# Half of the first modulation rows summed on TensorE, and the second modulation row of each chunk queued behind the weights

## The chip, the cores and the metric

The kernel runs on one core of a Trainium2 chip. The metric is the device time of one execution in microseconds; lower is better. TensorE (PE in the rows) multiplies matrices, VectorE (DVE), ScalarE (ACT) and GpSimd (POOL) do elementwise work, and SyncE (SP) issues the loads. Each engine runs its own program in order and waits on semaphores for the others.

## The reference

Two transformer blocks follow each other on x of 256 rows by 1024 columns. Each has a gated feed-forward (FFN), an attention mix and another FFN. Every normalised input is scaled and shifted by vectors ("modulation") that are themselves a product of a small vector with a large matrix:

```
mods = (silu(c) @ w_ada + b_ada).reshape(B, 9, 1024)      # w_ada: 1024 x 9216
n = rmsnorm(h, g_pre[0]) * (1 + scale(0)) + shift(0)
f = (silu(n @ w_gate) * (n @ w_up)) @ w_down              # 1024 x 2816, 1024 x 2816, 2816 x 1024
h = h + 0.5 * gate(0) * rmsnorm(f, g_post[0])
```

The first FFN can't start before shift(0) and scale(0) are there: 2048 columns of w_ada, 8 MB. The other modulation vectors of the first block are worked out during that FFN.

## The kernel before, in words

All matrices are float32. To get near-float32 results out of the faster float32r matmuls, each weight piece is split in two, hi (ScalarE copies with rounding) and lo = raw - hi (VectorE subtracts), and so is the activation nT. A product is then three matmuls, hi by hi, hi by lo and lo by hi. `split_hi` (ACT, L838) and `split_lo` (DVE, L1228) do this for a piece of 128 x 2048, which takes two loads of 512 KB.

An FFN is cut into 11 chunks of 256 hidden columns. Stage F0 is the first FFN. For chunk c TensorE multiplies piece (0, c), that is rows 0 to 511 of gate and up, then piece (1, c), rows 512 to 1023, and then the down piece of the chunk before. Pieces lie in four buffers (A = w_raw 0, B = 1, D = 2, E in the arena); `lo_ready` of a buffer tells SyncE that it may be loaded again and TensorE that it may be used.

The opening is written out by hand (`opening` on TensorE, `first_rows`, `first_fold`, `first_folded` and `first_out` on VectorE, `load_first` on SyncE). It works in two halves of 512 columns of shift and scale. Half 0 is needed for rows 0 to 511 of the FFN's weights, half 1 for rows 512 to 1023. For a half there are eight modulation rows (j = 0 to 7) of 128 x 1024, 512 KB each. A row is multiplied by the column `c_act[:, 0, j]` and added up; the sum over partitions and the turn into columns comes from a fold (DVE reduce, L1516) and one matmul with a constant, `pick` (L2133). VectorE sums all eight rows of half 0 and six of half 1. The other two rows of half 1 (`ON_PE = [2, 3]`) are summed on TensorE by `first_row_sums`: eight matmuls a row with the 128 x 128 block of the row as weights and one moving column (L2140), put between the weight matmuls three at a time behind one tile of chunk 0 and then one at a time in piece (0, 1). When `first_mods` says that a half's shift and scale are ready, the transposed x is scaled into nT (ACT L865, DVE L1251) and split. x is transposed on TensorE (L1950).

During F0, `load_ada` queues two modulation rows a chunk, 128 x 3072 and 1.5 MB each (ada 0 and ada 1), and VectorE multiplies and adds them (L1317, L1320). In the loop both are queued behind the down piece and ahead of the next chunk's gate and up pieces, and both are added ahead of their splits.

## Time and profile before

| | us |
|---|---|
| median of 3 runs | 1088.44 |
| lowest and highest | 1088.26, 1089.09 |
| the profiled execution | 1088.02 |
| its span | 1086.3 |
| TensorE busy in the span | 1057.0 |
| VectorE, ScalarE busy | 854.4, 549.7 |

The span is the time from the first to the last instruction that the profiler saw; 1.7 us of the execution lie outside of it. A busy TensorE is one that has a matmul in flight; it says nothing about how densely the matmuls follow each other, which one reads from their start times.

### The profile page before, as it was taken

How to read it: one execution, taken by the hardware profiler on the slowest of the kernel's cores; microseconds unless marked ns; L12 is line 12 of the kernel's file. 1: busy time of each engine (PE TensorE's matmuls, PEld its weight loads, DVE VectorE, ACT ScalarE, POOL GpSimd, SP SyncE). 2: the span in 40 equal slices, each digit the busy share in tenths (PEclk: the TensorE clock that was granted, in tenths of full speed). 3: DMA queues.
4: the chain of work that ended last, by engine and by line, in shares of the span. 5: the costliest groups of instructions: out<-in, count | busy, mean ns of one | idle time of the engine just before them, and what ended most of it. 6: DMA issues, size and time to landing. Idle time of an engine off the chain costs nothing.

```text
span 1086.3 us, 16196 instructions
## 1 busy us (share of the span) xinstructions
PE 1057.0 (97%) x6136; PEld 924.2 (85%) x6136; DVE 854.4 (79%) x932; ACT 549.7 (51%) x669; POOL 47.6 (4%) x78
## 2 busy tenths in 40 slices
PE   3999999999999999999999999999999999999997
PEld 2999999889988788888978888898887778888886
DVE  6899888678887888887778988877876787666665
ACT  4444343564765754444565444445654456444452
POOL 1000000011120100000010000000100000000001
PEclk9999999999999999999999999999999999999999
DMA  9999997466424598997669999854563536767651
GB/s 340 382 403 389 389 394 265 152 157 218 150 78 155 194 336 309 320 311 239 206 235 350 344 369 339 278 174 136 179 206 104 194 118 226 233 214 231 216 174 59
DMA packets 147140, 265.26 MB, mean 244 GB/s; under 512 B 9769, under 2 KB 104470, under 8 KB 141974
## 3 DMA queue, kind: packets, MB, share of 16 engines
q1 hardware_dynamic: 145376, 261.30, 69.7%
q0 software_dynamic: 1056, 3.17, 1.0%
q8 instruction: 30, 0.49, 0.2%
q10 hardware_dynamic: 662, 0.16, 0.1%
q14 instruction: 16, 0.13, 0.0%
HBM read 263.34 MB, written 1.27 MB: 244 GB/s over the span
## 4 chain that ended last, share of the span: by engine, by line
PE 90%; DVE 4%; ACT 2%; DMA 1%; issue 1%; SPq 1%; POOL 1%; POOLq 0%; DVEq 0%; ACTq 0%
PE ps L1999 18%; PE ps L1930 12%; PE ps L1931 12%; PE ps L1932 12%; PE ps L2005 9%; PE ps L1980 7%; PE ps L1982 6%; PE ps L1983 6%; DMA arena<-in_w_ffn_up 1%; ACT w_hi L838 1%; PE ps L2474 1%; DVE x_res L1405 1%; DVE nT L1251 1%; DVE y_row L1399 0%; PE ps L2293 0%
## 5 line engine op out<-in xcount | busy, mean ns | idle before, releaser
L1228 DVE TENSOR_TENSOR w_lo<-w_raw,w_hi 128x2048 fp32r<-128x2048 f32 (+1 forms) x163 | 367.1, 2254 | 103.3 <-ACT w_hi L838 102.5
L838 ACT ACTIVATE w_hi<-w_raw 128x2048 fp32r<-128x2048 f32 (+2 forms) x169 | 317.5, 1884 | 245.4 <-PE ps L1932 96.4
L1999 PE MATMUL ps<-nT_both,w_hi 128*128 128x512 f32 x864 | 210.7, 391 | 0.0
L1999 PEld LDWEIGHTS ps<-nT_both,w_hi 128*128 128x128 f32 x864 | 158.8, 188 | 30.7
L1980 PE MATMUL ps<-nT_both,w_hi 128*128 128x256 f32 x576 | 164.3, 285 | 0.0
L1982 PE MATMUL ps<-nT_both,w_hi 128*128 128x256 f32 x576 | 162.9, 283 | 0.0
L1983 PE MATMUL ps<-nT_both,w_lo 128*128 128x256 f32 x576 | 162.9, 283 | 0.0
L1320 DVE SCALAR_TENSOR_TENSOR arena<-arena,c_act 128x3072 f32<-128x3072 f32 (+2 forms) x49 | 129.4, 2651 | 0.4 <-DMA arena<-in_ada_w 0.4
L1930 PE MATMUL ps<-w_hi,hT_hi 128*128 128x512 f32 x320 | 125.0, 391 | 0.0
L1931 PE MATMUL ps<-w_lo,hT_hi 128*128 128x512 f32 x320 | 125.0, 390 | 0.0
L1932 PE MATMUL ps<-w_hi,hT_lo 128*128 128x512 f32 x320 | 124.5, 389 | 0.0
L2005 PEld LDWEIGHTS ps<-nT_both,w_lo 128*128 128x128 f32 x864 | 114.3, 191 | 6.3
L2005 PE MATMUL ps<-nT_both,w_lo 128*128 128x256 f32 x864 | 116.3, 282 | 0.0
L1980 PEld LDWEIGHTS ps<-nT_both,w_hi 128*128 128x128 f32 x576 | 110.4, 192 | 0.7
L1982 PEld LDWEIGHTS ps<-nT_both,w_hi 128*128 128x128 f32 x576 | 110.5, 192 | 0.4
L1983 PEld LDWEIGHTS ps<-nT_both,w_lo 128*128 128x128 f32 x576 | 110.4, 192 | 0.0
L1930 PE MATMUL ps<-w_hi,nT_both 128*128 128x512 f32 (+2 forms) x236 | 91.4, 387 | 0.1
L1932 PE MATMUL ps<-w_hi,nT_both 128*128 128x512 f32 (+2 forms) x236 | 89.7, 380 | 0.0
L1931 PE MATMUL ps<-w_lo,nT_both 128*128 128x512 f32 (+2 forms) x236 | 89.6, 380 | 0.0
L1932 PEld LDWEIGHTS ps<-w_hi,hT_lo 128*128 128x128 f32 x320 | 60.1, 188 | 12.8
L1930 PEld LDWEIGHTS ps<-w_hi,hT_hi 128*128 128x128 f32 x320 | 60.2, 188 | 11.4
L1931 PEld LDWEIGHTS ps<-w_lo,hT_hi 128*128 128x128 f32 x320 | 60.2, 188 | 11.0
(310 smaller groups left out, 1239.8 us busy)
## 6 DMA issues: line engine op xcount, KB each, us to landing
arena<-in_w_ada SPq DMA_DIRECT2D x16, 1536.0 KB, 9.4
arena<-in_ada_w SPq DMA_DIRECT2D x16, 1536.0 KB, 8.2
w_raw<-in_w_in SPq DMA_DIRECT2D x44, 512.0 KB, 4.5
w_raw<-in_ffn_w_down SPq DMA_DIRECT2D x44, 512.0 KB, 4.1
w_raw<-in_w_ffn_gate SPq DMA_DIRECT2D x42, 512.0 KB, 7.0
w_raw<-in_w_ffn_up SPq DMA_DIRECT2D x42, 512.0 KB, 8.2
w_raw<-in_w_ffn_down SPq DMA_DIRECT2D x42, 512.0 KB, 4.5
w_raw<-in_ffn_w_gate SPq DMA_DIRECT2D x42, 512.0 KB, 4.2
```

Of the source, the lines that this page charges most:

```text
L838: copy = lambda o, i: act.activation(o, i, ACT.Copy)
L1228: dve.tensor_tensor(lo(s, n), raw(s, n), hi(s, n).bitcast(F32), ALU.subtract).then_inc(lo_ready[s], 1)
L1251: dve.tensor_scalar(nT[:, k, t * P:(t + 1) * P], norm_at(f, t, pair, i), cols[:, 0, k:k + 1], cols[:, 1, k:k + 1], ALU.mult, ALU.add).then ...
L1320: dve.scalar_tensor_tensor(acc, ada_raw[:, half, 0:n], c_act[:, blk, bass.ds(j, 1)], acc, ALU.mult, ALU.add)\
L1930: pe.matmul(o, xh, wh, start=start, stop=False, skip_group_check=True)
L1931: pe.matmul(o, xh, wl, start=False, stop=False, skip_group_check=True)
L1932: return pe.matmul(o, xl, wh, start=False, stop=stop, skip_group_check=True)
L1980: pe.matmul(o, hi(s)[:, cols], nT_hi[:, kk, :], start=(half == first_half and k == 0 and i % 2 == 0), stop=False, skip_group_check=True)
L1982: pe.matmul(o, hi(s)[:, cols], nT_lo[:, kk, :], start=False, stop=False, skip_group_check=True)
L1983: last = pe.matmul(o, lo(s)[:, cols], nT_hi[:, kk, :], start=False, stop=(half != first_half and k == 3), skip_group_check=True)
L1999: pe.matmul(ps[:, i, :], hi(s)[:, cols], nT_both[:, 4 * half + k].rearrange("p a n -> p (a n)"), start=(half == 0 and k == 0), stop=False, ...
L2005: last = pe.matmul(ps[:, i, 0:S], lo(s)[:, cols], nT_hi[:, kk, :], start=False, stop=(kk == KD - 1), skip_group_check=True)
```

## The change

Three things change, all in stage F0. First, in both halves rows 0 to 3 are summed on VectorE and rows 4 to 7 on TensorE (`first_row`, 32 matmuls of one column a half, where before it was none and 16). The rows of half 0 stand on TensorE ahead of the weights; those of half 1 stand in piece (0, 1), three behind each of its last eight groups, with row 7 behind the fold. Second, the splits of the first piece of each half are cut in two and interleaved with the scaling of x, the first tile's matmuls take their operands in the order in which these come, and most of the scaling goes from ScalarE to VectorE. Two runs of matmuls whose result nobody reads (`spin`) stand on TensorE, 12 behind the first matmul and 5 behind `first_mods` of half 0. Third, ada 1 of each chunk is queued behind the next gate and up pieces and added behind the product h_act.

```
-        ON_DVE = [[0, 1, 2, 3, 4, 5, 6, 7], [0, 1, 4, 5, 6, 7]]
-        ON_PE = [2, 3]
+        ON_DVE = [0, 1, 2, 3]
+        ON_PE = [4, 5, 6, 7]
...
             if f == "F0":
-                return [(t, pair, i) for t, pair in HALF_PAIRS[:6] for i in range(2)]
+                return [(0, pair, i) for pair in (0, 2) for i in range(2)]
...
                 def chunk(c):
                     load_down(f, c - 1)
                     load_ada(f, 0, c - 1)
-                    load_ada(f, 1, c - 1)
+                    if f != "F0":
+                        load_ada(f, 1, c - 1)
                     load_gu(f, 0, c + 1)
                     load_gu(f, 1, c + 1)
+                    if f == "F0":
+                        load_ada(f, 1, c - 1)
...
             load_gu("F0", 0, 0)
+            load_gu("F0", 0, 1)
+            for j in range(2):
+                sp.wait_ge(first_sum, j + 1)
+                load_first(1, j)
             sp.wait_ge(toe_sb, 1)
             sp.dma_start(toe_dram.rearrange("(p n) -> p n", p=P), toe_rows).then_inc(toe_stored, 16)
-            for j in range(KD):
-                sp.wait_ge(first_sum, j + 1)
+            for j in range(2, KD):
+                if j in ON_DVE:
+                    sp.wait_ge(first_sum, j + 1)
+                else:
+                    sp.wait_ge(fold_mm, FOLDS.index("rows 0") + 1)
                 load_first(1, j)
...
+            def first_split(half):
+
+                s, use = gate_up("F0", half, 0)
+                a, b = 2 * half, 2 * half + 1
+                dve.wait_ge(first_mods, half + 1)
+                norm_cols("F0", 0, b)
+                norm_cols("F0", 1, a)
+                norm_lo("F0", 0, a)
+                norm_cols("F0", 1, b)
+                dve.wait_ge(first_hi, half + 1)
+                dve.tensor_tensor(lo(s)[:, 0:D], raw(s)[:, 0:D], hi(s)[:, 0:D].bitcast(F32), ALU.subtract).then_inc(first_lo, 1)
+                norm_lo("F0", 0, b)
...
+            def first_row(half, j):
+
+                pe.wait_ge(first_loaded[j], 16 * (half + 1))
+                for k in range(KD):
+                    last = pe.matmul(ps[:, fold_bank(f"rows {half}"), k:k + 1], first_at[half][j][:, k * P:(k + 1) * P],
+                                     c_act[:, 0, j:j + 1], start=(j == ON_PE[0] and k == 0), stop=(j == ON_PE[-1]),
+                                     skip_group_check=True)
...
+                    if half == 0:
+                        gate_up_half("F0", 0, 1, each=between)
+                        for _ in row_sums:
+                            pass
+                        first_fold(1)
+                        for _ in first_row(1, ON_PE[-1]):
+                            pass
...
+            for j in ON_PE:
+                if j == ON_PE[1]:
+                    first_fold(0)
+                if j == ON_PE[-1]:
+                    for t in range(T):
+                        norm_transposes("F0", t, range(2))
+                for _ in first_row(0, j):
+                    pass
             norm_transposes("F0", 0, range(2, PAIRS))
-            first_fold(0)
             pe.wait_ge(vec_ready, 2)
             norm_transposes("F0", 1, range(2, PAIRS))
-            pe.wait_ge(c_ready, 1)
+            pe.wait_ge(first_mods, 1)
+            spin(0, 5)
             ffn("F0")
```

How the order of instructions moves is shown at two places. The first is TensorE from the program's start up to the first weight matmuls. Before (L1950 transposes x, L2133 is the fold matmul, L1930 the first weight matmul):

```order
L2189 MATMUL ps<-arena 128x384
L2193 MATMUL ps<-ident,vec_rows 128x104
L2193 MATMUL ps<-ident,vec_rows 128x101
L1950 MATMUL ps<-ident,y_row 128x128 x12
L2133 MATMUL ps<-arena 128x32
L1950 MATMUL ps<-ident,y_row 128x128 x4
L1930 MATMUL ps<-e_hi,nT_both 128x512
```

Changed (L2222 are the spins, L2150 the row matmuls, L2144 the fold matmul, L1961 the transposes, L2183 and L2190 the first tile's weight matmuls):

```order
L2226 MATMUL ps<-arena 128x384
L2222 MATMUL ps<-ones,ident 128x128 x12
L2231 MATMUL ps<-ident,vec_rows 128x104
L2231 MATMUL ps<-ident,vec_rows 128x101
L2150 MATMUL ps<-c_act,arena 128x1 x8
L2144 MATMUL ps<-arena 128x32
L2150 MATMUL ps<-c_act,arena 128x1 x8
L2150 MATMUL ps<-c_act,gate 128x1 x8
L1961 MATMUL ps<-ident,y_row 128x128 x8
L2150 MATMUL ps<-c_act,gate 128x1 x8
L1961 MATMUL ps<-ident,y_row 128x128 x8
L2222 MATMUL ps<-ones,ident 128x128 x5
```

Four rows of half 0 now stand among the transposes, the last of them behind the transposes of both tiles; the fold matmul has moved ahead.

The second place is TensorE at the end of piece (0, 1), just ahead of piece (1, 0). Before, the last group of piece (0, 1) is followed at once by the matmuls of piece (1, 0):

```order
L1980 MATMUL ps<-nT_both,w_hi 128x256
L1982 MATMUL ps<-nT_both,w_hi 128x256
L1983 MATMUL ps<-nT_both,w_lo 128x256
L1930 MATMUL ps<-w_hi,nT_both 128x512
L1931 MATMUL ps<-w_lo,nT_both 128x512
L1932 MATMUL ps<-w_hi,nT_both 128x512
```

Changed (L1991, L1993 and L1994 are the same three matmuls of a group):

```order
L1991 MATMUL ps<-nT_both,w_hi 128x256
L1993 MATMUL ps<-nT_both,w_hi 128x256
L1994 MATMUL ps<-nT_both,w_lo 128x256
L2150 MATMUL ps<-c_act,arena 128x1 x3
L2144 MATMUL ps<-arena 128x32
L2150 MATMUL ps<-c_act,arena 128x1 x8
L2183 MATMUL ps<-w_hi,nT_both 128x512 x8
L2190 MATMUL ps<-w_lo,nT_both 128x512 x4
```

The fold of half 1, which stood behind the fifth group of piece (0, 1), now stands behind the sixteenth and last, and eight row matmuls stand between it and the weights of piece (1, 0).

## Rows read from the trace of the kernel before

**Rows 1.** The page: span, and busy time of the first engine

```profile
span 1086.3 us, 16196 instructions
PE 1057.0 (97%) x6136; PEld 924.2 (85%) x6136; DVE 854.4 (79%) x932; ACT 549.7 (51%) x669; POOL 47.6 (4%) x78
```

**Rows 2.** Busy us (instructions) by engine in four stretches, clock, DMA

```profile
3.20:37.80 34.60, 19.39 (x89) 15.24 (x90) 26.85 (x32) 13.90 (x24) 3.42 (x4) 1.00 1.07 375
25.23:223.40 198.17, 197.82 (x1334) 182.95 (x1334) 166.39 (x130) 88.89 (x93) 4.21 (x10) 1.00 0.91 334
25.23:30.23 5.00, 5.00 (x13) 3.95 (x13) 4.05 (x6) 3.57 (x6) 0.00 (x0) 1.00 1.07 381
60.00:162.00 102.00, 102.00 (x724) 96.25 (x723) 89.66 (x43) 40.88 (x31) 0.00 (x0) 1.00 1.04 393
```

**Rows 3.** TensorE in order of time: start, duration, instruction, idle before

```profile
7.35 1.61 PE L2189 MATMUL ps<-arena 32*128 32x384 f32 x2 [7.35 <-DVE arena L1493]
13.14 0.60 PE L2193 MATMUL ps<-ident,vec_rows 104*128 104x104 f32 x2 [4.18 <-DMA vec_rows<-in_kv_norm]
18.43 1.97 PE L1950 MATMUL ps<-ident,y_row 128*128 128x128 f32 x8 [0.52 <-ACT y_row L991]
25.23 0.77 PE L1930 MATMUL ps<-e_hi,nT_both 128*128 128x512 f32 x1 [2.90 <-DVE nT_both L1258]
...
30.23 0.40 PE L1930 MATMUL ps<-e_hi,nT_both 128*128 128x512 f32 x1
...
30.92 0.72 PE L2140 MATMUL ps<-c_act,arena 128*128 128x1 f32 x6
...
32.29 0.73 PE L2140 MATMUL ps<-c_act,arena 128*128 128x1 f32 x6
...
38.36 0.30 PE L2133 MATMUL ps<-arena 128*128 128x32 f32 x2
...
42.58 0.47 PE L1930 MATMUL ps<-w_hi,nT_both 128*128 128x512 f32 x1
...
48.11 0.28 PE L1980 MATMUL ps<-nT_both,w_hi 128*128 128x256 f32 x1
...
93.71 0.28 PE L1980 MATMUL ps<-nT_both,w_hi 128*128 128x256 f32 x1
```

**Rows 4.** VectorE in order of time

```profile
8.55 4.06 DVE L1511 SCALAR_TENSOR_TENSOR arena<-arena,c_act 128x1024 f32<-128x1024 f32 x3
...
16.77 2.67 DVE L1511 SCALAR_TENSOR_TENSOR arena<-gate,c_act,arena 128x1024 f32<-128x1024 f32 x2
19.48 1.25 DVE L1516 TRANSPOSE_TENSOR_REDUCE arena<-arena 128x32 f32<-128x1024 f32 x1
...
22.18 0.16 DVE L1537 SCALAR_TENSOR_TENSOR mod_col<-mod_col,vec_col 128x4 f32<-128x4 f32 x1
22.45 2.29 DVE L1228 TENSOR_TENSOR e_lo<-arena,e_hi 128x2048 fp32r<-128x2048 f32 x1
...
88.94 2.29 DVE L1228 TENSOR_TENSOR w_lo<-w_raw,w_hi 128x2048 fp32r<-128x2048 f32 x1 [0.45 <-ACT w_hi L838]
```

**Rows 5.** ScalarE in order of time

```profile
17.22 1.15 ACT L991 ACTIVATE y_row<-x_res,stat 128x1024 f32<-128x1024 f32 x1 [0.55 <-POOL stat L764]
20.51 1.91 ACT L838 ACTIVATE e_hi<-arena 128x2048 fp32r<-128x2048 f32 x1 [2.14 <-DMA arena<-in_w_ffn_up]
22.38 0.81 ACT L865 ACTIVATE nT<-ps,mod_col 128x128 f32<-128x128 f32 x2
23.21 0.42 ACT L838 ACTIVATE nT_both<-nT 128x256 fp32r<-128x256 f32 x1
...
37.86 1.91 ACT L838 ACTIVATE w_hi<-w_raw 128x2048 fp32r<-128x2048 f32 x1 [8.99 <-DMA w_raw<-in_w_ffn_up]
```

**Rows 6.** SyncE's issues of the first ada row and of piece (1, 2)

```profile
38.15 1.50 SPq L593 DMA_DIRECT2D arena<-in_w_ada  x1
47.39 0.37 SPq L575 DMA_DIRECT2D w_raw<-in_w_ffn_gate  x1
```

More of the change, by code:

```diff
@@ L281, in program @@
         }
-        FOLDS = ["first 0", "rows 1", "first 1", "F0", "F0 late", "F1", "F2", "F2 late", "F3"]
+        FOLDS = ["first 0", "rows 0", "first 1", "rows 1", "F0", "F0 late", "F1", "F2", "F2 late", "F3"]
         fold_cols = {
@@ L1324, in body @@
                 i = FFN.index(f) * NC
-                opening = f == "F0" and isinstance(c, int) and c < 3
+                late = mods and f == "F0"
                 if mods and wide(f, c):
@@ L1334, in body @@
                         ada(f, 0, c - 1)
-                    if not opening:
+                    if not late:
                         ada(f, 1, c - 1)
@@ L1558, in _ @@
             first_out(1)
[L1559 to L1566 removed]
+            first_split(1)
             ffn("F0", piece1(0, 0))
@@ L2153, in opening, with between @@
+            def first_row_sums():
+                for j in ON_PE[:-1]:
+                    yield from first_row(1, j)
+            def opening():
+                row_sums, called = first_row_sums(), itertools.count()
+                def between():
+                    if next(called) >= 8:
+                        for _ in range(3):
+                            next(row_sums, None)
                 for half in range(2):
                     s, use = gate_up("F0", half, 0)
-                    weights(s, use)
@@ L2156, in opening @@
-                    for t in range(T):
-                        for k in range(4):
-                            last = row_group(s, o, NB, "F0", 4 * half, start=(half == 0), stop=(half == 1), tiles=(t,), ks=[k])
-                            if half == 0 and t:
-                                if k == 3:
-                                    last.then_inc(w_used[s], 1)
-                                for _ in range(3):
-                                    next(row_sums)
-                        if half and t == 0:
-                            last.then_inc(row_mm, 1)
@@ L2166, in opening @@
-                    if half == 0:
-                        gate_up_half("F0", 0, 1, each=lambda: next(row_sums, None))
-                    else:
-                        last.then_inc(w_used[s], 1)
+                    o = [ps[:, t, :] for t in range(T)]
+                    for part in range(2):
+                        pair = 2 * half + part
+                        if part:
+                            pe.wait_ge(hi_ready[s], use + 1)
+                        else:
+                            pe.wait_ge(first_hi, half + 1)
+                        for x, ready in ((nT_hi, n_hi), (nT_lo, n_lo)):
+                            pe.wait_ge(ready, pair_count("F0", 0, pair))
+                            for k in (2 * part, 2 * part + 1):
+                                pe.matmul(o[0], x[:, 4 * half + k, 0:P], hi(s)[:, k * NB:(k + 1) * NB],
+                                          start=(half == 0 and k == 0 and ready is n_hi), stop=False, skip_group_check=True)
@@ new lines, in opening @@
+                    for k in range(4):
+                        if k == 0:
+                            pe.wait_ge(first_lo, half + 1)
+                        if k == 2:
+                            weights(s, use)
+                        last = pe.matmul(o[0], nT_hi[:, 4 * half + k, 0:P], lo(s)[:, k * NB:(k + 1) * NB],
+                                         start=False, stop=(half == 1 and k == 3), skip_group_check=True)
+                    if half:
+                        last.then_inc(row_mm, 1)
@@ L2184, in ffn, with spin @@
                 last_downs(f)
+            def spin(bank, n):
+                for _ in range(n):
+                    pe.matmul(ps[:, bank, 0:P], ident[:], ones[:], start=True, stop=True, skip_group_check=True)
             pe.wait_ge(const_ready, 2)
```

110 lines of the change are left out of this document (44 added, 66 removed).

## The prediction

> **What bounds the kernel now.** I read the page first: TensorE is busy for 1057.0 of a span of 1086.3 us [rows 1], so little can be won outside of what TensorE does and of the 29 us in which it doesn't. The stretches come next: from its first weight matmul at 25.23 us to the end of stage F0 at 223.4 us TensorE is busy for 197.82 of 198.17 us [rows 2]. So a microsecond gained or lost in the opening goes through to the end of F0, and the later stages take it over as a shift. The timeline of TensorE shows the rest: the first weight matmul waited 2.90 us for VectorE [rows 3], and the chain to it is short. Piece (0, 0) landed at 20.5 (ScalarE waited for it), hi took until 22.42, lo until 24.74 [rows 4, 5], a small split of x followed, and TensorE started. The memory side is full meanwhile: 375 GB/s from 3.2 to 37.8 us, DMA share 1.07 [rows 2]. At that rate a load of 512 KB takes 1.4 us, and the order of the queue sets every landing. Piece (1, 0) landed at 37.8 [rows 5] and TensorE wanted it at 42.58, when piece (0, 1) ended [rows 3].
>
> Twelve weight matmuls lie between 25.23 and 30.23 us, 0.42 us apart, where later 24 of the same form take 42.58 to 48.11, 0.23 apart [rows 3]. The granted clock stands at 1.00 in this stretch too [rows 2]; the spacing says the lower level (1.2 GHz) until about 30 us, after TensorE had done transposes with gaps, and the higher (2.4 GHz) from then on. That cost 12 x 0.23 = 2.8 against 5.0, so 2.2 us.
>
> **What the change can give.** In place of summing row 7 on VectorE (until 19.44 [rows 4]), folding (1.25), and only then adding, the fold comes early and row 7 comes last on TensorE. I follow half 0. TensorE ends its first matmul at 8.96, the vector transposes at 13.74 [rows 3]; the 12 spins (0.43 us each at the low clock, by 128 columns in four passes, as the 384 columns of the first matmul took 1.61) end at 13 to 14. A row on TensorE is eight matmuls. Three of them, placed between others, cost 32.29 - 30.92 = 1.37 us less three weight matmuls of 0.23, that is 0.68, 0.23 each [rows 3]. Back to back, I take 0.19 (six records in 0.72 us, with the tail of the last one in flight), 1.5 us a row. Rows 4, 5 and 6 then end near 15.3, 17.0 and 18.5. The transposes of both tiles stand ahead of row 7; tile 1 has its input at 18.37 [rows 5], so they end at 19.5 and row 7 at 21.0. VectorE adds and finishes with `first_mods` at 21.4. On ScalarE come now 0.8 us scaling, 0.4 split of x [rows 5], and half of the weight split, half of 1.91 and a fixed part, 1.05: the first weight matmul can go at 23.9, 1.3 us earlier than 25.23. With the clock up by the spins, the 2.2 us are saved too. The tile's operands then come one after another (VectorE has three pairs of scalings, two half splits of 1.17 and the small splits between 21.4 and 26.6), which makes 12 matmuls take 3.2 instead of 2.8: 0.4 lost.
>
> **What it costs.** TensorE's work between its first weight matmul and piece (1, 1) is 48.11 - 25.23 = 22.9 us now [rows 3]. In it are 16 row matmuls: four threes (2.7) and four singles of 0.22, 3.6. Without these and without the 2.2 of the low clock it is 17.1. The change puts 32 in: eight threes, 5.4, and row 7's eight, 1.6 with the switch, 7.0 together. So 3.4 us more work on the engine that is never idle there. VectorE, which gives the rows up, had room: its work before piece (1, 0) is done by 42 either way.
>
> Then a wait is new. Before, the fold of half 1 is done at 38.4 [rows 3], behind the fifth of 16 groups of piece (0, 1), and the scaling, the split of piece (1, 0) (landed at 37.8) and of x run behind the other eleven, which take 42.58 - 38.50 = 4.1 us, 0.37 each. Now row 7 and the fold stand behind the last group. Behind row 7 TensorE has nothing queued that it may do: VectorE's two small instructions (0.16 each [rows 4], 0.4 with the hop), ScalarE's scaling (0.8), split of x (0.4) and half weight split (1.05), with the hops 2.8 us, pass with TensorE idle. The first tile is fed piecewise again, 0.5.
>
> In order: 23.9 (start) + 6.2 (piece (0, 0), with 0.4 and hops) = 30.1; piece (0, 1) 16 x 0.37 = 5.9 and 5.4 of rows, 41.3; fold and row 7, 43.1; idle to 45.9; piece (1, 0) 5.5 + 0.5, so piece (1, 1) at 51.8. Before it was 48.11. **The sum is +3.7 us.** As a check by terms: -1.3 - 2.2 + 0.4 + 3.4 + 2.8 + 0.5 = +3.6.
>
> One term has bounds far apart: what the clock does while TensorE works on one-column matmuls, transposes and waits, from 13 to 24 us. No row shows one-column matmuls alone. Nearest below is the stretch from 30.92 on, in which half of TensorE's time is such matmuls and the spacing of the others stays 0.23; nearest above is the stretch ahead of 25.23, transposes and gaps, behind which the spacing is 0.42. Below, the term is nothing. Above, each of the last two or three rows takes up to twice its 1.5 us, the transposes 1.97 instead of half of it [rows 3], and the first weight matmuls go at the low level again: up to +5. I take a small part, +0.8 (half of row 7's doubling), since spins run before and behind.
>
> **The Trainium skill** has a rule that would speak for a cheaper row: "TensorE: Matmul & The Clock Gate", section "Architectural detail: the array is 16× 32×32, not 1× 128×128", says that TensorE can pull a weight load ahead of matmuls in flight. By it the loads of the interleaved rows would hide behind their neighbours and the 5.4 us would go towards nothing; by the rows it is 0.68 a three, and I keep that.
>
> The third part, ada 1 behind the weights, I cost at nothing for TensorE. In the loop it never waits in before. Its tightest piece is (0, 4): VectorE ends lo at 91.23 [rows 4] and TensorE wants it at 93.71 [rows 3], 2.5 us to spare. A chunk loads 6.3 MB in 17 us, 370 of the 393 GB/s of the loop [rows 2], so queueing 1.5 MB behind gate and up lets these land about 4 us earlier, and ada 1 is then the last to land, with VectorE's split of (1, c+1) behind it, which TensorE wants 5.8 us later than (0, c+1). The cover is those 5.8 us; without it each microsecond of lateness would be paid once. On SyncE the first ada load and all behind it wait for "rows 1", which comes at 43.1 instead of 38.15 [rows 6], and piece (1, 2) waits for lo of (1, 1), near 52 instead of 47.39. The queue holds loads until about 46 and, with the ada row, 50.5; so about 3 us of the memory's time are lost, in step with TensorE's own 3.7.
>
> **The forecast** is +3.7 + 0.8 = +4.5 us on an execution of 1088.02, whose span is 1086.3; the median is 0.4 above that execution, so 1088.44 + 4.5 = 1092.9.
>
> **Rivals.** *The clock is lost (chance 0.2).* If one-column matmuls let it fall, row 7 ends at 23 to 25, the start is behind 26, the first weights are at 0.42 again, and the wait of 2.8 us before piece (1, 0) lets it fall a second time. That is +7 to +9, 1096. For it: twelve slow matmuls behind transposes. Against: the spins.
>
> *The opening comes out level (0.1).* If row 7 is summed as soon as it lands (VectorE took it up at 18.1, so by 20.0), the first weight matmul goes at 22.5 and nothing waits piecewise: +3.7 - 1.4 - 0.9 = +1.4, 1089.8. Against it stand tile 1's transposes at 18.37.
>
> *Row sums cost TensorE almost nothing (0.08), faster.* The mechanism is weight loads hidden behind streaming neighbours in piece (0, 1). At no cost for the threes the piece ends at 35.9, VectorE's fold (four rows from 30 on, 36) binds, and piece (1, 0), landed at 37.8, gets its first hi half by 39: TensorE starts it at 39.1 instead of 42.58 and with 0.5 of piecewise feeding the end is -3.0, 1085.4. It decides from a row term of half its size on: 45.9 has to come down by 3.8 of the 7.0 us. The 0.68 a three speaks against it.
>
> *The late queue starves F0 (0.07).* If the 3 us of idle queue and the later ada 1 use up the 2.5 us to spare, TensorE waits once or more in the loop: another +2 to +4, 1096. For it: 370 of 393 GB/s are asked for. Against: gate and up land earlier.
>
> **How the numbers follow.** The forecast has 0.55. Its own range, from the pieces' bounds, is 1091.2 to 1094.5. The rivals reach 1096 and more above, and 1089.8 and 1085.4 below; leaving out the faster one and the tail above 1097 gives 1089.6 to 1097.0. A measurement here tells about 0.2%, 2.2 us, from no change. Slower by more is the forecast, both slow rivals and nothing of the level one: 0.82. Within 0.2%: 0.1. Faster: 0.08.
>
> **What would show it.** In the profile of the changed kernel: the first L2183 matmul at 23 to 25 us; weight matmuls 0.23 apart from there on (clock up) or 0.42 (rival); piece (0, 1) lasting 11 us instead of 7; an idle TensorE of about 2.8 us, released by ScalarE's hi, at 43 to 46; piece (1, 1) near 52; no wait of TensorE from there to the end of F0, whose end moves from 223.4 to about 228. The forecast is wrong if the last one-column matmul ends well before 41, if the second wait is absent, or if the chunks of the loop are longer than 17.0 us.

## The result, and the profile after

| | before | changed |
|---|---|---|
| median us (runs) | 1088.35 (4) | 1104.27 (4) |
| lowest, highest | 1088.21, 1089.09 | 1102.35, 1104.99 |
| the profiled execution | 1088.02 | 1102.35 |
| its span | 1086.3 | 1100.6 |

The ratio is 1.0142, 95% interval 1.0125 to 1.016. So the change costs 15.9 us of the median, where 4.5 were forecast, and the time lies 7 us above the widest range stated (1097.0). The profiled execution is the fastest of the four changed ones; its span is 14.3 us longer than before, and that is what the rows below explain. Two of the eleven executions of a kernel further down, before_spins_late, took 1508 and 2128 us, and no reading uses them.

The page of the changed kernel, the lines that answer to [rows 1]:

```profile
span 1100.6 us, 16456 instructions
PE 1078.9 (98%) x6266; PEld 947.8 (86%) x6266; DVE 849.9 (77%) x937; ACT 546.1 (50%) x663; POOL 45.9 (4%) x78
```

TensorE is busy for 21.9 us more, though only 130 matmul records came in: 17 spins and 48 row matmuls, two records each. Busy time by engine in stretches of the changed kernel, columns as in [rows 2] (PE, PEld, DVE, ACT, POOL, clock, DMA share, GB/s):

```profile
3.20:37.80 34.60, 30.12 (x174) 27.89 (x174) 19.36 (x33) 11.36 (x19) 1.60 (x4) 0.85 1.06 370
20.00:30.00 10.00, 10.00 (x48) 9.83 (x49) 4.69 (x12) 4.34 (x9) 0.00 (x0) 0.55 1.07 380
40.00:50.00 10.00, 10.00 (x60) 10.00 (x59) 0.65 (x4) 0.00 (x0) 0.00 (x0) 0.63 0.64 229
50.00:60.00 10.00, 7.24 (x23) 6.01 (x23) 7.77 (x15) 5.89 (x10) 0.00 (x0) 0.52 0.43 158
62.50:237.76 175.26, 174.91 (x1205) 162.63 (x1203) 146.75 (x102) 78.01 (x76) 4.20 (x9) 1.00 0.88 325
```

The last row first: from piece (1, 1) to the end of F0 the changed kernel takes 175.26 us; before, the same work went from 48.11 [rows 3] to 223.40 [rows 2], 175.29 us. The rest of F0 neither lost nor won anything, and what comes behind F0 takes 862.8 us against 862.9. All of the loss of this execution lies ahead of piece (1, 1), and there the granted clock stands at 0.55, 0.63 and 0.52 in three stretches: TensorE spent them mostly at 1.2 GHz, in the second one while it was busy throughout.

TensorE in order of time, changed kernel (answers to [rows 3]; L2222 spins, L2150 row matmuls, L1961 transposes, L2144 fold, L2183 and L2190 first-tile weights; "threes" below are the three row matmuls behind a group, "level" is the higher or the lower of the two clocks):

```profile
9.03 4.28 PE L2222 MATMUL ps<-ones,ident 128*128 128x128 f32 x24
...
13.78 1.92 PE L2150 MATMUL ps<-c_act,arena 128*128 128x1 f32 x16 [0.20 <-DMA arena<-in_w_ada]
...
17.57 2.54 PE L2150 MATMUL ps<-c_act,gate 128*128 128x1 f32 x16
19.98 1.95 PE L1961 MATMUL ps<-ident,y_row 128*128 128x128 f32 x8
21.72 3.41 PE L2150 MATMUL ps<-c_act,gate 128*128 128x1 f32 x16
...
26.73 2.33 PE L2222 MATMUL ps<-ones,ident 128*128 128x128 f32 x10
28.73 2.17 PE L2183 MATMUL ps<-e_hi,nT_both 128*128 128x512 f32 x8
...
40.67 0.72 PE L2150 MATMUL ps<-c_act,arena 128*128 128x1 f32 x6
...
41.70 0.72 PE L2150 MATMUL ps<-c_act,arena 128*128 128x1 f32 x6
...
42.83 1.27 PE L2150 MATMUL ps<-c_act,arena 128*128 128x1 f32 x6
...
47.80 0.61 PE L2144 MATMUL ps<-arena 128*128 128x32 f32 x2
48.23 3.55 PE L2150 MATMUL ps<-c_act,arena 128*128 128x1 f32 x16
54.54 3.78 PE L2183 MATMUL ps<-w_hi,nT_both 128*128 128x512 f32 x8 [2.76 <-ACT w_hi L845]
58.12 1.79 PE L2190 MATMUL ps<-w_lo,nT_both 128*128 128x512 f32 x4
```

A float32 matmul leaves two records, so x16 is one modulation row. Row 4 takes 1.92 us, row 7 takes 3.41: the same eight matmuls at either level of the clock, 0.22 us each and 0.41 to 0.43. The level falls within row 6, at 18.7 us by the granted clock, and comes back at 28.9, just behind the first weight matmul. It falls again at 42.6, within the threes of piece (0, 1), where 0.72 turns into 1.27; it stays low through row 7, and the first twelve weight matmuls of piece (1, 0) are 0.43 apart as well. The wait of 2.76 us stands at 51.8 to 54.5.

VectorE at the two last sums of shift and scale (answers to [rows 4]):

```profile
25.24 0.16 DVE L1542 TENSOR_TENSOR mod_col<-mod_col,ps 128x8 f32<-128x8 f32 x1 [8.49 <-PE ps L2150]
...
51.89 0.16 DVE L1542 TENSOR_TENSOR mod_col<-mod_col,ps 128x8 f32<-128x8 f32 x1 [2.75 <-PE ps L2150]
```

ScalarE behind them (answers to [rows 5]):

```profile
25.63 0.81 ACT L872 ACTIVATE nT<-ps,mod_col 128x128 f32<-128x128 f32 x2 [9.11 <-DVE mod_col L1544]
...
26.79 1.04 ACT L845 ACTIVATE e_hi<-arena 128x1024 fp32r<-128x1024 f32 x1
...
53.45 1.04 ACT L845 ACTIVATE w_hi<-w_raw 128x1024 fp32r<-128x1024 f32 x1
```

SyncE's issues of the first ada row and of piece (1, 2) (answers to [rows 6]):

```profile
51.87 0.34 SPq L592 DMA_DIRECT2D arena<-in_w_ada  x1
60.50 0.37 SPq L574 DMA_DIRECT2D w_raw<-in_w_ffn_gate  x1
```

Both other engines stand idle for 8.5 and 9.1 us until TensorE's row 7 of half 0 is there, so TensorE's slow matmuls are on the path, and nothing hides them. ScalarE's first half of hi is done at 27.8, but TensorE is still at its five spins, at the low level, and the weights start only behind them, at 28.73. SyncE issues both loads 13 to 14 us later than before [rows 6], in step with TensorE.

### The profile page after: what moved, and what is told of

The parts are those of the page before. It is cut to its first block, busy times and chain, and to the rows that moved or that the text cites. A ratio compares the mean times of both kernels' runs of the same rounds, so it can differ in the third digit from the quotient of the medians.

```text
span 1100.6 us, 16456 instructions
## 1 busy us (share of the span) xinstructions
PE 1078.9 (98%) x6266; PEld 947.8 (86%) x6266; DVE 849.9 (77%) x937; ACT 546.1 (50%) x663; POOL 45.9 (4%) x78
## 3 DMA queue, kind: packets, MB, share of 16 engines
HBM read 263.34 MB, written 1.27 MB: 240 GB/s over the span
## 4 chain that ended last, share of the span: by engine, by line
PE 90%; DVE 4%; ACT 3%; issue 1%; DMA 1%; POOL 1%; SPq 0%; POOLq 0%; DVEq 0%; ACTq 0%
PE ps L2010 18%; PE ps L1941 12%; PE ps L1942 11%; PE ps L1943 11%; PE ps L2016 9%; PE ps L1991 6%; PE ps L1994 6%; PE ps L1993 6%; PE ps L2150 2%; ACT w_hi L845 1%; DMA arena<-in_w_ada 1%; PE ps L2519 1%; DVE x_res L1412 1%; PE ps L1961 1%; PE ps L2183 1%
## 5 line engine op out<-in xcount | busy, mean ns | idle before, releaser
L1235 DVE TENSOR_TENSOR w_lo<-w_raw,w_hi 128x2048 fp32r<-128x2048 f32 (+3 forms) x162 | 364.8, 2254 | 91.1 <-ACT w_hi L845 90.5
L1991 PE MATMUL ps<-nT_both,w_hi 128*128 128x256 f32 x576 | 164.7, 286 | 0.0
L1994 PE MATMUL ps<-nT_both,w_lo 128*128 128x256 f32 x576 | 163.3, 284 | 0.0
L1993 PE MATMUL ps<-nT_both,w_hi 128*128 128x256 f32 x576 | 163.3, 283 | 0.0
L1991 PEld LDWEIGHTS ps<-nT_both,w_hi 128*128 128x128 f32 x576 | 110.7, 192 | 0.8
L1993 PEld LDWEIGHTS ps<-nT_both,w_hi 128*128 128x128 f32 x576 | 110.7, 192 | 0.4
L1994 PEld LDWEIGHTS ps<-nT_both,w_lo 128*128 128x128 f32 x576 | 110.8, 192 | 0.0
L1941 PE MATMUL ps<-w_hi,nT_both 128*128 128x512 f32 (+2 forms) x232 | 89.8, 387 | 0.1
L1943 PE MATMUL ps<-w_hi,nT_both 128*128 128x512 f32 (+2 forms) x232 | 88.1, 380 | 0.0
```

The source lines that it names most:

```text
L1235: dve.tensor_tensor(lo(s, n), raw(s, n), hi(s, n).bitcast(F32), ALU.subtract).then_inc(lo_ready[s], 1)
L1941: pe.matmul(o, xh, wh, start=start, stop=False, skip_group_check=True)
L1943: return pe.matmul(o, xl, wh, start=False, stop=stop, skip_group_check=True)
L1991: pe.matmul(o, hi(s)[:, cols], nT_hi[:, kk, :], start=(half == first_half and k == 0 and i % 2 == 0), stop=False, skip_group_check=True)
L1993: pe.matmul(o, hi(s)[:, cols], nT_lo[:, kk, :], start=False, stop=False, skip_group_check=True)
L1994: last = pe.matmul(o, lo(s)[:, cols], nT_hi[:, kk, :], start=False, stop=(half != first_half and k == 3), skip_group_check=True)
```

## The experiments

The table has the changed kernel and twelve others beside the one before. It gives the places of TensorE's milestones, in us from the span's start of each profiled execution, then the median and the ratio to before. "Last row matmul ends" is the end of what stands right ahead of piece (1, 0) where that is a row matmul; in half1_back it is the last group. In mended_change four groups follow it.

| kernel | first weights | piece (0, 1) | last row matmul ends | piece (1, 0) | piece (1, 1) | median | ratio (95%) |
|---|---|---|---|---|---|---|---|
| before | 25.23 | 35.60 | - | 42.58 | 48.11 | 1088.2 | 1 |
| changed | 28.73 | 34.35 | 51.8 | 54.54 | 62.50 | 1104.27 | 1.0142 (1.0125-1.016) |
| wide64 | 25.94 | 32.0 | 45.25 | 48.00 | 55.49 | 1095.23 | 1.0064 (1.0047-1.0081) |
| wide64_spin2 | 25.54 | 31.6 | 44.86 | 47.63 | 53.7 | 1093.32 | 1.0046 (1.0031-1.0061) |
| wide64_early | 25.34 | 31.4 | 45.0 | 47.8 | 54.8 | 1095.46 | 1.0069 (1.0053-1.0084) |
| no_rows_half1 | 30.86 | 36.99 | 44.81 | 47.6 | 55.5 | 1095.02 | 1.0057 (1.004-1.0074) |
| half1_back | 30.99 | 39.18 | 46.45 | 49.07 | 55.13 | 1095.73 | 1.0074 (1.0057-1.0091) |
| half0_back | 24.4 | 30.9 | 47.5 | 50.3 | 57.4 | 1098.01 | 1.0099 (1.0084-1.0115) |
| rows_early | 28.68 | 34.4 | 47.6 | 50.32 | 58.8 | 1100.27 | 1.0113 (1.0099-1.0128) |
| no_spins | 32.28 | 39.5 | 58.4 | 61.15 | 69.2 | 1109.34 | 1.0195 (1.018-1.021) |
| late_ada_alone | 25.43 | 35.1 | - | 42.80 | 48.3 | 1088.12 | 1.0001 (0.9991-1.001) |
| before_spins | 25.27 | 35.0 | - | 43.82 | 49.4 | 1089.84 | 1.0016 (1.0007-1.0026) |
| before_spins_late | 25.37 | 34.3 | - | 43.88 | 49.4 | 1089.38 | 1.0009 (0.9999-1.0018) |
| mended_change | 23.91 | 34.22 | 41.6 | 43.49 | 50.41 | 1090.25 | 1.0035 (1.0018-1.0051) |

**Is it the clock or the work?** Two kernels tell it. In the first the work stays and the matmuls get wider:

```
+        WIDE = 64
...
-                    last = pe.matmul(ps[:, fold_bank(f"rows {half}"), k:k + 1], first_at[half][j][:, k * P:(k + 1) * P],
-                                     c_act[:, 0, j:j + 1], start=(j == ON_PE[0] and k == 0), stop=(j == ON_PE[-1]),
+                    last = pe.matmul(ps[:, fold_bank(f"rows {half}"), k * WIDE:(k + 1) * WIDE], first_at[half][j][:, k * P:(k + 1) * P],
+                                     c_act[:, 0, j:j + 1].broadcast_to([P, WIDE]), start=(j == ON_PE[0] and k == 0),
...
```

VectorE reads one of the 64 equal columns. In half 1 the sums of the rows and of the fold also swap their PSUM banks here (4 and 5), which the second kernel doesn't do.

> The changed kernel, with 64 equal moving columns instead of one in every row matmul (the same weights, the same number of matmuls, results in 64 columns of which one is read). Theory clock: one-column matmuls let TensorE's clock fall to the lower level, and each of the drops is paid in slower rows, groups and weight matmuls. Then the wider ones keep it up: spacing 0.23 us throughout, piece (0, 1) 11 us instead of 13.4, row 7 of half 1 under 2 us instead of 3.6, first weights near 24.5 instead of 28.7, and the time near 1094 (1091 to 1096). Theory work: the matmuls are dear by themselves (weight loads of blocks that the queue fills at the same time); then nothing changes, 1103 to 1106, and spacing falls to 0.42 as before.

It gave 9.0 us back with the same number of matmuls and more columns. A row takes 1.9 to 2.1 us at every place, row 7 too, and the granted clock stands at 1.00 up to the wait. In the second kernel the 24 row matmuls of half 1 that stand between groups are left out, so that the scale and shift of columns 512 to 1023 miss rows 4 to 6:

```
             def first_row_sums():
 
-                for j in ON_PE[:-1]:
-                    yield from first_row(1, j)
+                return iter(())
...
-                                     c_act[:, 0, j:j + 1], start=(j == ON_PE[0] and k == 0), stop=(j == ON_PE[-1]),
+                                     c_act[:, 0, j:j + 1], start=(k == 0 and (half == 1 or j == ON_PE[0])), stop=(j == ON_PE[-1]),
```

> The changed kernel without the 24 interleaved row matmuls of half 1: rows 4, 5 and 6 of that half are left out of the sum, row 7 stays. Theory work alone: 24 matmuls at 0.23 are gone, 5.4 us, 1098.9. Theory clock: piece (0, 1) takes 5.8 instead of 13.4 us (5.4 of work, 2.3 of clock), row 7 runs at the higher level (2 us less), the 12 first weight matmuls of piece (1, 0) too (2 us less) unless the idle 2.8 us alone let the clock fall: 1092.3, or 1094.4 if they do.

TensorE at row 7 of half 1 and at the first tile of piece (1, 0) in this kernel:

```profile
42.88 1.93 PE L2150 MATMUL ps<-c_act,arena 128*128 128x1 f32 x16
47.56 3.78 PE L2182 MATMUL ps<-w_hi,nT_both 128*128 128x512 f32 x8 [2.76 <-ACT w_hi L845]
```

It gave 9.2 us back, though the 24 matmuls are worth 5.5 us at the high level, and though its weights started 2.1 us later than in the profiled changed kernel. Row 7 takes 1.93 us where it took 3.55. The code of half 0 is the same as in the changed kernel, but the level rose later in this execution: the twelve spins took 5.3 us instead of 4.2, the rows stood 1.1 us later, and all of row 6 fell into the low level (from 18.5 us on). The changed kernel's other three runs, 1.7 to 2.6 us above its profiled one, may well be such ones, but they have no trace.

**Does the wait lower the clock too?** wide64 kept the level through all its rows. Then it waited 2.75 us for ScalarE's hi, the granted clock fell at 49.2 us, 1.2 us behind the end of the wait, and came back at 52.6:

```profile
48.00 3.33 PE L2184 MATMUL ps<-w_hi,nT_both 128*128 128x512 f32 x8 [2.75 <-ACT w_hi L846]
51.13 1.76 PE L2191 MATMUL ps<-w_lo,nT_both 128*128 128x512 f32 x4
```

So ten spins were put into that wait:

```
                         for _ in first_row(1, ON_PE[-1]):
                             pass
+                        pe.wait_ge(first_mods, 2)
+                        spin(5, 10)
```

> wide64 with ten more spins on TensorE behind first_mods of half 1, which fill the last 2.1 of the 2.75 us in which it waits for the first split of piece (1, 0). If the idle time is what lets the clock fall there, the first matmuls of piece (1, 0) come 0.23 instead of 0.42 us apart and 1.5 us are won over wide64: 1093.7. If the fall has another cause, 1095.2 again or more.

TensorE's timeline in this kernel (L2156 row matmuls, L2150 the fold, L2144 spins, L2189 first-tile weights):

```profile
42.07 0.78 PE L2156 MATMUL ps<-c_act,arena 128*128 128x64 f32 x6
42.68 0.36 PE L2150 MATMUL ps<-arena 128*128 128x32 f32 x2
42.88 1.98 PE L2156 MATMUL ps<-c_act,arena 128*128 128x64 f32 x16
45.38 2.50 PE L2144 MATMUL ps<-ones,ident 128*128 128x128 f32 x20 [0.52 <-DVE mod_col L1545]
47.63 2.42 PE L2189 MATMUL ps<-w_hi,nT_both 128*128 128x512 f32 x8
```

Two of its stretches, by engine, with the granted clock:

```profile
40.00:50.00 10.00, 9.41 (x73) 8.59 (x72) 5.61 (x16) 4.61 (x9) 0.00 (x0) 1.00 0.99 359
50.00:60.00 10.00, 10.00 (x70) 9.02 (x69) 7.87 (x9) 6.10 (x6) 0.00 (x0) 1.00 0.59 192
```

The level holds throughout, x16 takes 1.98 where the changed kernel had 3.55, and x8 of the first weights 2.42 where it had 3.78. The spins fill the wait and shorten it by nothing: piece (1, 0) starts 2.77 us after row 7. Another 1.9 us of the median came back, 1.4 of it in piece (1, 0). This kernel is the changed one with the clock kept from row 4 on, and so the one against which the other terms of the forecast can be read. (Its twelve spins ran at the low level to their end, 14.28 us, where those of the changed kernel's profiled execution ended at 13.19.)

**Does it matter where the rows stand?** Two kernels put two row matmuls behind each of the sixteen groups, row 7 too, and the fold behind the fourteenth; once with one column, once with 64:

```
                 def between():
-                    if next(called) >= 8:
-                        for _ in range(3):
-                            next(row_sums, None)
+                    i = next(called)
+                    for _ in range(2):
+                        next(row_sums, None)
+                    if i == 13:
+                        first_fold(1)
```

> The changed kernel with the 32 one-column row matmuls of half 1 put two behind each of the 16 groups of piece (0, 1), row 7 too, and the fold behind the fourteenth group, so that no eight of them stand alone ahead of the wait. Theory clock by density: one-column matmuls take TensorE to the low level from the first groups on, since nothing denser stands between; piece (0, 1) takes as long or longer than before (13 to 17 us), row 7 no longer costs 3.5 us by itself, the wait is 2.8 us again: 1101 to 1106. Theory that only the standing-alone row 7 and the wait cost the clock: twos between groups cost 0.46 each at the high level, the piece ends near 47.5, 1097 to 1099.

> wide64 with the rows of half 1 spread, two matmuls behind each of the 16 groups of piece (0, 1), fold behind the fourteenth group; the last row sum still ends with the piece. The same 32 matmuls, less switching: piece and rows take 13.0 instead of 13.2 us; the wait of 2.75 us stays. If the clock falls behind row 7's own block of matmuls, it doesn't fall here: 1093.5. If the wait alone does it: 1095.

rows_early, TensorE from piece (0, 1) to its first tile of piece (1, 0):

```profile
34.79 0.50 PE L2150 MATMUL ps<-c_act,arena 128*128 128x1 f32 x4
...
47.06 0.50 PE L2150 MATMUL ps<-c_act,arena 128*128 128x1 f32 x4
50.32 3.78 PE L2185 MATMUL ps<-w_hi,nT_both 128*128 128x512 f32 x8 [2.75 <-ACT w_hi L845]
```

The same kernel's stretch of piece (0, 1), by engine:

```profile
34.40:47.60 13.20, 13.16 (x115) 13.04 (x114) 5.80 (x9) 0.00 (x0) 0.00 (x0) 1.00 0.91 310
```

All sixteen pairs take 0.50, so the 32 matmuls of one column no longer take the level down, and row 7 costs no more than the others: 4.3 us came back in the trace (34.35 to 51.8 has become 34.4 to 47.6), 4.0 in the median. I had expected either the level lost from the first groups on, or 1097 to 1099; the first is refuted, and the second was too low, for the level still falls in the wait (at 49.6 us), and half 0 is as slow as in the changed kernel. wide64_early says the same of the wait alone: it kept 1.00 until 47.0 us, inside its wait of 2.75 us, and its piece (1, 0) took 7.0 us where it took 6.1 with spins in the wait.

**Either half undone.** In half1_back the rows of half 1 are shared out as in the kernel before, rows 2 and 3 on TensorE, and the fold stands behind the fourteenth group, where before it stood behind the fifth; the split of piece (1, 0) in two parts stays. In half0_back half 0 is as before, with no row on TensorE:

```
-ON_DVE = [0, 1, 2, 3]                  # half1_back
-ON_PE = [4, 5, 6, 7]
+ON_DVE = [[0, 1, 2, 3], [0, 1, 4, 5, 6, 7]]
+ON_PE = [[4, 5, 6, 7], [2, 3]]
...
-ON_DVE = [0, 1, 2, 3]                  # half0_back
+ON_DVE = [[0, 1, 2, 3, 4, 5, 6, 7], [0, 1, 2, 3]]
```

> The changed kernel with half 1 as before: six rows on VectorE, rows 2 and 3 on TensorE, three a group behind tile 1 and then one a group; the fold stands behind the fourteenth group. Half 0, splits, spins and queue stay as changed. Theory clock plus wait: the second drop (42.5 to 59.7 us), 16 row matmuls and the idle 2.8 us go, piece (1, 1) starts near 51 instead of 62.5: 1092 to 1094, the rest over 1088.4 being half 0. If half 0 were the main cost: 1098 or more.

> The changed kernel with half 0 as before on VectorE (all eight rows; transposes, then the fold); splits, spins, half 1 and queue stay as changed. By the clock account half 0's rows cost the changed kernel 4 us of start (28.7 against about 24.9 here), but half 1 keeps its fall of the clock, its 32 row matmuls and its wait: first weights near 25, piece (0, 1) near 31.5, piece (1, 1) near 59.5, and 1100.5 to 1102.5. If half 0 were the main cost instead: 1094 or less.

Half 1 alone is worth 8.5 us of the 15.9 and half 0 alone 6.3, as medians; the rest is in neither alone. Both forecasts were missed. half0_back came out at 1098.0, not at 1100.5 or more: its level fell one three later than the changed kernel's and its piece (1, 0) took 7.1 us instead of 8.0. half1_back came out at 1095.7, not at 1092 to 1094: its wait stayed, and in its execution the level fell at 17.1 us, within row 5, so that its weights start at 31.0.

half0_back starts its weights at 24.4, 4.3 us ahead of the changed kernel, for no row stands on TensorE ahead of them. The level is low there too: the granted clock fell at 16.0 us, in a wait of 2.89 us behind the spins, and came back at 26.3, so that most of the first eight weight matmuls ran at the low level. Its threes fell to the low level too, at 40.0 us; this loss is half 1's own.

half1_back, the first tile of piece (1, 0):

```profile
49.07 2.44 PE L2184 MATMUL ps<-w_hi,nT_both 128*128 128x512 f32 x8 [2.62 <-ACT w_hi L845]
```

It waited 2.62 us and kept the clock at 1.00 from 40 to 60 us. Groups with no row matmul between them had run right up to its wait. In no_rows_half1 sixteen such groups ran too, but row 7's eight one-column matmuls stood between them and the wait of 2.76 us, and there the level fell, at 45.8 us. What makes the difference, these eight matmuls, the 0.14 us more of waiting or the moment in the execution, no run separates.

**The spins of the change.** Without both runs of spins:

```
-            spin(2, 12)
...
             pe.wait_ge(first_mods, 1)
-            spin(0, 5)
             ffn("F0")
```

> The changed kernel without both runs of spins, 12 behind the first matmul and 5 behind first_mods of half 0. In the changed kernel the twelve end only at 14.3 us, at the low level, so rows 4 and 5 can start some 0.5 us earlier, and the five are no part of the path either way (they run while the first weight split is awaited). Theory clock (what TensorE did just before sets the level of the matmuls that follow): without the five spins the first weight matmuls start at 0.42 apart and stay there longer, rows 4 to 6 as slow or slower; piece (1, 1) starts 0.5 to 2.5 us later than 62.5, so 1103 to 1106. Theory work (spins are only more work on TensorE in the opening, and the time of the changed kernel is that of its matmuls): 0.5 to 1 us less, 1101.5 to 1102.

TensorE in this kernel:

```profile
13.67 3.54 PE L2150 MATMUL ps<-c_act,arena 128*128 128x1 f32 x16
17.08 0.61 PE L2144 MATMUL ps<-arena 128*128 128x32 f32 x2
17.50 3.55 PE L2150 MATMUL ps<-c_act,arena 128*128 128x1 f32 x16
20.92 3.55 PE L2150 MATMUL ps<-c_act,gate 128*128 128x1 f32 x16
...
26.07 3.41 PE L2150 MATMUL ps<-c_act,gate 128*128 128x1 f32 x16
```

Every row of half 0 is at the low level from the first one on, and the weights start at 32.28. That is 5 us worse, twice what I had allowed for. So the spins do lift the level (row 4 in 1.92 us instead of 3.54), and in the changed kernel's profiled execution it lasts for two rows and a half. I had taken the five spins to be off the path either way; in the changed kernel they cost 0.9 us, since they ran at the low level, and without them the weights wait 0.99 us for ScalarE's hi. Note the clock column for the same kernel: it reads 1.00 from 10 to 30 us here,

```profile
20.00:30.00 10.00, 10.00 (x48) 10.00 (x49) 0.34 (x3) 0.01 (x1) 0.00 (x0) 1.00 0.92 323
```

while x16 takes 3.55. The kernel before has the same ahead of 30 us [rows 2]. In both the level had not been up yet; in the kernels in which spins had raised it once, the column agrees with the spacing from there on.

**The third part alone**, on the kernel before: ada 1 of each chunk queued behind the gate and up pieces and added behind h_act, in F0.

```
                     load_down(f, c - 1)
                     load_ada(f, 0, c - 1)
-                    load_ada(f, 1, c - 1)
+                    if f != "F0":
+                        load_ada(f, 1, c - 1)
                     load_gu(f, 0, c + 1)
                     load_gu(f, 1, c + 1)
+                    if f == "F0":
+                        load_ada(f, 1, c - 1)
...
-                opening = f == "F0" and isinstance(c, int) and c < 3
+                opening = mods and f == "F0"
```

> The kernel before with the third part alone: in stage F0 ada 1 is queued behind the gate and up pieces and added behind h_act. Forecast: nothing, 1088.1 to 1088.8, no wait of TensorE in the loop. Theory starved queue: TensorE waits in the loop, 1089.5 or more.

Nothing, within 0.1%, as forecast.

**Is the clock worth anything to the kernel before?** It loses 2.2 us to the low level at its first weights. Six spins behind the vector transposes and six ahead of the weights were tried, and then the latter alone:

```
+            spin(2, 6)      # before_spins only
             pe.wait_ge(pick_ready, 1)
...
             pe.wait_ge(c_ready, 1)
+            spin(2, 6)      # both
             ffn("F0")
```

> The kernel before with 6 spins behind the vector transposes and 6 behind the last transposes of x, nothing else. The 2.2 us that the low clock costs from 25.2 to 30.2 us shrink. Theory of a second bound: TensorE then comes to piece (1, 0) early and waits for VectorE's lo, which ended at 42.1 us before and hangs on a load that lands at 37.8: no gain, 1088.0 to 1088.4, with a wait of 1 us or more near 41.5. Theory of the work bound: 1086.0 to 1086.8.

> The kernel before with six spins directly ahead of its first weight matmul only, none behind the vector transposes. It tells whether the later landing of piece (1, 0) with twelve spins comes with spins in general. If the spins lift the level for the first weight matmuls, these end 1 to 2 us earlier and piece (1, 0) is awaited from about 41 on; with the landing of before (hi from 37.86, lo until 42) the result is 1087.4 to 1088.2, and the opening is bound by lo of piece (1, 0) and not by the clock. If the landing is late again, 1088.5 to 1090.

before_spins_late, TensorE at the fifteenth weight matmul of piece (0, 0), which went at 30.70 before, and at the start of piece (1, 0):

```profile
29.43 0.39 PE L1932 MATMUL ps<-e_hi,nT_both 128*128 128x512 f32 x1
...
43.88 0.47 PE L1930 MATMUL ps<-w_hi,nT_both 128*128 128x512 f32 x1 [1.41 <-DVE nT_both L1258]
```

ScalarE's hi of piece (1, 0) in it:

```profile
39.17 1.91 ACT L838 ACTIVATE w_hi<-w_raw 128x2048 fp32r<-128x2048 f32 x1 [10.13 <-DMA w_raw<-in_w_ffn_up]
```

The spins right ahead of the weights work: piece (0, 1) starts 1.3 us earlier than before (34.3 against 35.60). In before_spins it starts 0.6 us earlier only. There the level had risen by the first spins, the second ones ended 2.35 us ahead of the weights, and the granted clock fell again at 26.5 and stayed low until 29.9. Then, in before_spins_late, TensorE waits 1.41 us, because piece (1, 0) bounds the opening from the other side, and this piece landed at 39.17 instead of 37.86 [rows 5]. The landing was late in both kernels with spins, from an issue at most 0.2 us later and at nearly the same GB/s from 30 to 40 us (367 and 368, before 367). In late_ada_alone, without spins, the load was issued 0.3 us later than before and landed at 38.08. Why it was late with spins stays open. No gain was measured; before_spins_late is level with before, before_spins 0.16% slower.

**The change mended by what was learned:** rows of 64 columns, 9 spins, half 1 with three rows on TensorE (three matmuls behind each step of tile 1 in piece (0, 0), then one behind a group), the fold behind the eleventh group with the last two row matmuls behind it, hi of each first piece split ahead of the scaling:

```
+        ON_DVE = [[0, 1, 2, 3], [0, 1, 5, 6, 7]]
+        ON_PE = [[4, 5, 6, 7], [2, 3, 4]]
...
-                act.wait_ge(first_mods, half + 1)
-                norm_hi("F0", 0, [2 * half])
                 act.wait_ge(raw_loaded[s], use * 32 + 32)
                 copy(hi(s)[:, 0:D], raw(s)[:, 0:D]).then_inc(first_hi, 1)
-                norm_hi("F0", 0, [2 * half + 1])
                 copy(hi(s)[:, D:PIECE], raw(s)[:, D:PIECE]).then_inc(hi_ready[s], 1)
+                act.wait_ge(first_mods, half + 1)
+                norm_hi("F0", 0, [2 * half])
+                norm_hi("F0", 0, [2 * half + 1])
```

> The changed kernel mended by what the runs before showed: row matmuls of 64 equal columns (keep the level up), 9 spins in place of 12, half 1 with five rows on VectorE and three on TensorE, one behind each group, the fold behind the tenth group as before, no row behind the fold, and ScalarE's hi split of the first piece of each half ahead of the scaling. Expected by the ledger: start 25.3 to 25.8, piece (0, 1) at 31.5, its sixteen groups with 12 to 16 rows at 0.23 until 41 to 41.5, then piece (1, 0) bound by its landing at 37.8 and lo until about 42.3, piece (1, 1) at 47.5 to 49. So 1087.5 to 1089.5, level with before; a gain of more than 1 us would show that the half on TensorE is worth something once the clock holds, a loss of more than 2 us that a wait was overlooked.

TensorE at the first tile of either half:

```profile
23.91 1.62 PE L2185 MATMUL ps<-e_hi,nT_both 128*128 128x512 f32 x6
26.39 0.73 PE L2185 MATMUL ps<-e_hi,nT_both 128*128 128x512 f32 x2 [0.86 <-DVE nT_both L1266]
...
43.49 1.63 PE L2185 MATMUL ps<-w_hi,nT_both 128*128 128x512 f32 x6 [0.43 <-ACT nT_both L846]
45.97 0.73 PE L2185 MATMUL ps<-w_hi,nT_both 128*128 128x512 f32 x2 [0.85 <-DVE nT_both L1266]
```

It takes back 14.0 of the 15.9 us and is still 0.35% slower than before. Three of its twelve executions took 1097.1 to 1097.3 us, 7 us more than the other nine (1089.8 to 1090.4); none of the three has a trace, and what they waited for is not known. The weights start 1.3 us earlier than before. Piece (1, 0) starts 0.9 us later, for 24 instead of 16 row matmuls stand ahead of it and piece (1, 0) lands late here too (39.2), and it then takes 6.9 us instead of 5.5, since its first tile is fed piece by piece. The forecast had been 1087.5 to 1089.5. No kernel of this study beats the one before.

## Why the prediction was wrong

The direction was right and so was the place, the opening and nothing else. The size was wrong, nearly all of it by one term. Read beside the forecast's own milestones (wide64_spin2 is the changed kernel with the clock kept):

| | forecast | changed | wide64_spin2 |
|---|---|---|---|
| first weights | 23.9 | 28.73 | 25.54 |
| piece (0, 1) starts | 30.1 | 34.35 | 31.6 |
| its groups and rows end | 41.3 | 47.8 | 42.7 |
| fold and row 7 end | 43.1 | 51.8 | 44.86 |
| piece (1, 0) starts | 45.9 | 54.54 | 47.63 |
| piece (1, 1) starts | 51.8 | 62.50 | 53.7 |

**The step that failed** is the clock term: "I take a small part, +0.8 (half of row 7's doubling), since spins run before and behind". By the difference of the last two columns it is 62.5 - 53.7 = 8.8 us, and by the medians of the two kernels (1104.27 and 1093.32) 11.0 of the 15.9. The 8.8 are 3.2 until the first weights, 2.4 in piece (0, 1) with its threes (13.45 against 11.1), 1.8 in the fold and row 7 (4.0 against 2.2), nothing in the wait, 1.9 in piece (1, 0) (7.96 against 6.1), with 0.5 given back in piece (0, 0). Of the 3.2, 2.3 are there when row 7 ends (row 6 in part, the first transposes, row 7), and 0.9 is the time by which the five spins, behind the second transposes, outlast the wait for hi. The 3.2 are rather too low, for wide64_spin2's first spins ended 1.1 us later. Two things were wrong in it. I took the nearest row for the lower bound, [rows 3] at 30.92, threes between weight matmuls of 512 columns, and let it stand for threes between groups of 256 columns as well; in the changed kernel the level fell in those. And I bounded the term for half 0 alone, "up to +5", though row 7 of half 1 and the wait behind it were written down two paragraphs earlier as eight one-column matmuls followed by 2.8 us of nothing. The rival "the clock is lost" had the mechanism, and its +7 to +9 was still half of the loss. It had the first fall right (row 7 ended at 25.1), but the level was back for the first weights, 0.25 us apart, and the second fall came at 42.6, 9 us ahead of the wait: so it left out piece (0, 1) and row 7 of half 1, 4.2 us together.

**The start** was short by 1.6 us with the clock kept (25.54 for 23.9). Back to back a row takes 0.22 to 0.24 a matmul, not the 0.19 that I read from six records with the last tail in flight: four rows are 1.1 us longer. The rest is the twelve spins, which ended at 14.3 in wide64_spin2, above the 13 to 14 of the forecast, so that row 4 started 0.7 us late.

**More work on TensorE** held: wide64_spin2 takes 11.1 us for piece (0, 1) with its 24 row matmuls, forecast 11.2. **The new wait** held: 2.76 us, forecast 2.8, released by ScalarE's hi. **The piecewise feeding** held: 6.1 us for piece (1, 0), forecast 6.0. **The third part** cost nothing alone, and in the changed kernel the rest of F0 is as long as before. Taken together the forecast without its clock term was +3.7 and wide64_spin2 measures +5.6 at piece (1, 1), the 1.6 of the start being most of the difference.

**The rivals.** "The opening comes out level" is refuted even with the clock kept. "Row sums cost TensorE almost nothing" is refuted by the threes: in the changed kernel they follow each other 1.03 us apart (40.67 to 41.70), a group without one lasts 0.36, so a three costs 0.67, forecast 0.68. "The late queue starves F0" is refuted by 175.26 against 175.29 us.

## What to carry to other kernels

Small matmuls on TensorE are priced at two levels, and the step between them can be larger than all the rest of a change; wherever a change puts a run of tiny matmuls or a new wait on TensorE, price what stands behind it at both levels, at each such place, and not only at the first. A row of the trace that shows tiny matmuls at the high level vouches for its own neighbours only. When work is taken from an engine with slack and given to the engine that is never idle, ask first how late its last piece ends there; the 2.8 us of wait and the 3.4 us of work were visible in the order of the instructions, and would have sufficed to leave the change alone.

## What the runs showed of the hardware

- The same eight matmuls of one column took 1.78 us at the high level and 3.41 at the low (x16 with the tail 1.92 and 3.55). With 64 equal columns instead of one they took 1.90 to 1.98 with the tail, and the level held: 9 us for a wider operand that computes nothing more.
- With threes of one column between groups of 256 columns the level fell in the changed kernel, in half0_back and in no_spins (at 42.6, 40.0 and 46.0 us), with TensorE busy throughout; with twos behind all sixteen groups it did not, nor with threes between matmuls of 512 columns.
- An idle TensorE of 2.75 us was followed by the low level in four kernels that had been at the high one until then: the granted clock fell within the wait in wide64_early, rows_early and no_rows_half1, and 1.2 us behind it in wide64. In before_spins it fell 1.2 us behind a wait of 2.35 us, in half0_back within one of 2.89 us. In half1_back, with groups and no row matmul right before a wait of 2.62 us, it didn't, nor where spins filled the wait.
- The granted clock read 1.00 as long as the level had not risen once, at the spacing of the low level (x16 in 3.55 us).
- The same instructions of half 0 met the level at different places from one kernel to another. It fell within row 5 in half1_back (17.1 us), at the end of row 5 in no_rows_half1 (18.5) and within row 6 in the changed kernel (18.7), and twelve equal spins took 4.2 us in one and 5.3 in another (first weights at 28.7 to 31.0); the changed kernel's four runs spread over 2.6 us, those of before over 0.9.
- Left open: why piece (1, 0) landed 1.2 to 1.3 us later with spins on TensorE in the kernel before, and why three executions of mended_change took 7 us more.
